# Sums of the norms by ones times the split total, and means by a masked sum on DVE

## The chip, the cores and the metric

One core of a Trainium2 chip runs the whole program. The metric is the device time of one execution in microseconds, as the median of several runs. The engines are named as in the profile: PE (TensorE, matrix products; PEld is its weight load), DVE (VectorE), ACT (ScalarE), POOL (GpSimd) and SP (SyncE, which issues the DMAs).

## What is computed

Two layers over 256 tokens of 1024 channels. Each layer has four residual steps, and each step starts with an RMS norm of x; a fifth norm stands behind the last layer:

```python
def rmsnorm(x, g):
    y = x * lax.rsqrt(jnp.mean(x * x, axis=-1, keepdims=True) + EPS)
    return y * g

for i in range(DEPTH):                                     # DEPTH = 2
    x = x + 0.5 * swiglu(rmsnorm(x, norm_ff1[i]), ...)     # norm 0, D_FF = 2816
    x = x + token_mixer(rmsnorm(x, norm_mix[i]), ...)      # norm 1: sparse attention and gated linear attention
    x = x + 0.5 * swiglu(rmsnorm(x, norm_ff2[i]), ...)     # norm 2
    g = sigmoid(rmsnorm(x, norm_ple[i]) @ ple_w_gate[i])   # norm 3
    x = x + g * (p[i] @ ple_w_proj[i])
return rmsnorm(x, norm_final)
```

All is float32, and 216 MB of weights are read once.

## The kernel before

x lies transposed in SBUF: channels on the 128 partitions, eight tiles of 128 x 256 tokens. The weights come in chunks of 128x2048 (1 MB) through three slots. For each chunk SP loads `raw`, ACT rounds it into `w_hi` (float32r, `split` at line 856), DVE puts the remainder into `w_lo` (`split` at line 1222), and PE makes three products of each pair of tiles, hi with hi, lo with hi, hi with lo (lines 385 to 387). x times the gain is split in the same way (lines 876 and 1248). A chunk's slot is used again for the chunk three further on, so the instruction `split(L, n + 3)` appears beside the work on chunk n. Each engine runs its own list of instructions in the order written; semaphores connect the lists.

The factor 1/rms of a token is not needed before the products: they run on x times gain, and their results are multiplied by `rb`, a 128x256 tile that holds each token's factor on all partitions. A norm k of layer L makes `rb` so:

1. ACT squares the tiles of x in pairs (line 866), POOL adds the eight squared tiles into `total` (128x256, lines 1149 and 1150) and counts `sq_added`.
2. PE, in `token_sums`, waits for `sq_added` and sums `total` over the partitions: two float32 products with `total` as the stationary operand and one column of ones, so that a token's sum stands on a partition, in 128x2 of PSUM (line 424).
3. DVE, in `mean_square`, makes `mean` of it (line 1261), POOL raises it to the power -1/2 (`rstd`, line 1152), and DVE puts the two halves of `rstd` on diagonals, split as `diag_hi` and `diag_lo` (lines 1267 and 1270).
4. PE, in `spread`, multiplies `ones_r` (128x128 ones) with both diagonals, 256 columns each (lines 434 and 435); ACT copies the result into `rb` (line 892).

Where the steps stand on PE: in norm 0 of layer 0 (`first`) the sums come in the third chunk, after its first column tile; in norms 0 and 2 otherwise within the second chunk; in norm 1 between the two chunks of `av`; in norm 3 behind the chunk of `PROJ`. Where they stand on DVE: in norms 0 and 2, `mean_square` comes between `split(L, n + 3)` and `split(L, n + 4)` of the first pair of chunks; in norms 1 and 3 it comes at the end of the feed-forward stage before, at its last chunk (c = 10), after the last `rest_pair` and ahead of that chunk's `split(L, n + 3)`.

Of the kernel before, what the change touches and what calls it, by code (L numbers as in the profile page):

```python
# [7 lines left out]
F32 = mybir.dt.float32  # L8
F32R = mybir.dt.float32r
ACT = mybir.ActivationFunctionType  # L10
ALU = mybir.AluOpType
AX_X = mybir.AxisListType.X

P = 128
EPS = 1e-6
# [17 lines left out]
T = 256  # L33
D = 1024
# [53 lines left out]
def hybrid_trunk(nc, a, out):  # L88
    L_N = a["gla_gate_w2"].shape[0]
    with ExitStack() as ctx:  # L90
        def sb(name, shape, dt=F32):

            line = 16
            held = ctx.enter_context(nc.sbuf_tensor(name, [*shape[:-1], -(-shape[-1] // line) * line], dt))
            return held[(slice(None),) * (len(shape) - 1) + (slice(0, shape[-1]),)]

        def sem(name):
            return ctx.enter_context(nc.semaphore(name))

        psum = ctx.enter_context(nc.psum_tensor("psum", [P, 8, 512], F32))  # L100
        bank = [psum[:, b, :] for b in range(8)]
# [19 lines left out]
        total = sb("total", [P, T])  # L121
        diag_hi = sb("diag_hi", [P, 2, P], F32R)
        diag_lo = sb("diag_lo", [P, 2, P], F32R)
        diag = total.rearrange("p (a t) -> p a t", a=2)
        ones_r = sb("ones_r", [P, P], F32R)
        ones = ones_r.bitcast(F32)
        w2 = sb("w2", [P, 256])
# [16 lines left out]
        mean = sb("mean", [P, 2])  # L144
# [50 lines left out]
        ident = consts[:, 0:P]  # L195
# [3 lines left out]
        def both(t):  # L199

            return t.unsqueeze(1).to_broadcast([P, 2, t.shape[-1]])
# [25 lines left out]
        sq_done = sem("sq_done")  # L227
        sq_added = sem("sq_added")
        sums_done = sem("sums_done")
        mean_done = sem("mean_done")  # L230
        rstd_done = sem("rstd_done")
        diag_rounded = sem("diag_rounded")
# [53 lines left out]
        START = 1  # L286
# [9 lines left out]
        def turn(L, n, g=0):  # L296

            return n % SLOTS, L * TURNS + n // SLOTS + g + 1
# [14 lines left out]
        def of_norm(L, k, pair):  # L313

            return (L * 4 + k) * 4 + pair
# [60 lines left out]
        def _(pe):  # L376
# [42 lines left out]

            def token_sums(L, k, b):  # L420

                pe.wait_ge(sq_added, of_norm(L, k, 4) + START)
                for t in range(2):
                    mm = pe.matmul(bank[b][:, T + t:T + t + 1], total[:, t * P:(t + 1) * P], ones[:, 0:1], start=True, stop=True)  # L424
                mm.then_inc(sums_done, 1)

            def spread(L, k, b):

# [9 lines left out]
            def ffn(L, off, f, h):  # L438
# [14 lines left out]
                for m in range(4):  # L453
                    if m == 3 and not first:
                        token_sums(L, k, 4)
                    if f == 0:
                        if m < 3:
                            pe.wait_ge(next_lo, L * 3 + m + 1)
                        else:
                            operands(L, off + 1)  # L460
                    for c in range(2):
                        mm = pairs(s, 2, h, c, (2 * m, 2 * m + 1))
# [367 lines left out]
            for c in range(3):  # L830
                if c:
                    pe.wait_ge(last_squares, c)
                for t in range(2):
                    half = slice(t * P, (t + 1) * P)
                    mm = pe.matmul(bank[4][:, T + t:T + t + 1], last_squared[:, c - 1, half] if c else total[:, half], ones[:, 0:1],
                                   start=c == 0 and t == 0, stop=c == 2, skip_group_check=True)
# [372 lines left out]
        def _(dve):  # L1209
# [8 lines left out]
            def split(L, n, g=0):  # L1218

                s, t = turn(L, n, g)  # L1220
                dve.wait_ge(hi_ready[s], t)
                dve.tensor_tensor(w_lo[:, s, :], raw[:, s, :], w_hi[:, s, :].bitcast(F32), ALU.subtract).then_inc(lo_ready[s], 1)  # L1222

            def chunk_products(L, n, g=0):
                s, t = turn(L, n, g)
                dve.wait_ge(chunk_done[s], t + START)
# [17 lines left out]
            def rest_pair(L, k, m, h):  # L1244

                dve.wait_ge(h_hi_ready, of_norm(L, k, m + 1))
                for c in (2 * m, 2 * m + 1):
                    ins = dve.scalar_tensor_tensor(out=h[1][:, c, :], in0=x[:, c, :], scalar=gains[:, k, c:c + 1],
                                                   in1=h[0][:, c, :].bitcast(F32), op0=ALU.mult, op1=ALU.subtract)
                ins.then_inc(h_ready, 1)  # L1250

            def add_half(L, m, first):

                xs = x[:, 2 * m:2 * m + 2, :]
                dve.scalar_tensor_tensor(out=xs, in0=high(first), scalar=0.5, in1=xs, op0=ALU.mult, op1=ALU.add
                                         ).then_inc(x_done, 1)

            def mean_square(L, k, b):

                dve.wait_ge(sums_done, L * 4 + k + 1)  # L1260
                dve.tensor_scalar(mean[:, :], bank[b][:, T:T + 2], 1.0 / D, EPS, ALU.mult, ALU.add).then_inc(mean_done, 1)
                dve.wait_ge(rstd_done, L * 4 + k + 1)
                roots = rstd[:, :].unsqueeze(2).to_broadcast([P, 2, P])
                if L * 4 + k == L_N * 4:
                    dve.tensor_tensor(diag[:, :, :], both(ident), roots, ALU.mult).then_inc(diag_done, 1)
                    return
                dve.tensor_tensor(diag_hi[:, :, :], both(ident), roots, ALU.mult).then_inc(diag_rounded, 1)
                dve.wait_ge(diag_rounded, L * 4 + k + 1)
                for t in range(2):
                    ins = dve.scalar_tensor_tensor(out=diag_lo[:, t, :], in0=ident, scalar=rstd[:, t:t + 1],  # L1270
                                                   in1=diag_hi[:, t, :].bitcast(F32), op0=ALU.mult, op1=ALU.subtract)
                ins.then_inc(diag_done, 1)

            def products(q):
                return high(2 * q) if q < 2 else tiles(UP_BANKS[(q - 2) % 6])

            def ffn(L, off, f, k, h):
                F = L * 22 + f * 11
                for g in range(N_FF):
                    n = off + 2 * g  # L1280
                    if g == 0:
                        split(L, n + 3)
                        if L == 0 and f == 0:
                            dve.wait_ge(const_landed, 16)
                        mean_square(L, 2 * f, 4)
                        split(L, n + 4)
                        dve.wait_ge(rb_ready, L * 4 + 2 * f + 1)
                    chunk_products(L, n)
                    dve.tensor_tensor(gate_sum, products(2 * g), both(rb), ALU.mult).then_inc(gate_scaled, 1)
                    if g:  # L1290
                        split(L, n + 3)
                    chunk_products(L, n + 1)
                    dve.tensor_tensor(up_sum, products(2 * g + 1), both(rb), ALU.mult).then_inc(up_scaled, 1)  # L1293
                    dve.wait_ge(up_scaled, F + g + 1)
                    dve.wait_ge(silu_done, F + g + 1)
                    dve.tensor_tensor(gated_up, up_sum, gate_act, ALU.mult).then_inc(hidden_done, 1)
                    if g:
                        split(L, n + 4)
                    dve.wait_ge(hidden_hi, F + g + 1)
                    dve.tensor_tensor(hid[1][:, 2 * g:2 * g + 2, :], gated_up, hid[0][:, 2 * g:2 * g + 2, :].bitcast(F32),  # L1300
                                      ALU.subtract).then_inc(hidden_lo, 1)
                for c in range(N_FF):
                    n = off + DOWN + c
                    if c in (2, 5, 8, 10):
                        m = (2, 5, 8, 10).index(c)
                        if m < 3:
                            dve.wait_ge(acc_ready, L * 6 + 3 * f + m + 1)
                        else:
                            chunk_products(L, n)
                        add_half(L, m, DOWN_BANKS[m])  # L1310
                        rest_pair(L, k, m, h)
                        if m == 3:
                            mean_square(L, k, 6 if f == 0 else 7)
                    split(L, n + 3)
                    if f == 1 and c == 0:
                        dve.wait_ge(p_hi, L + 1)
                        dve.tensor_tensor(small_lo[:, 2, :], p_in, small_hi[:, 2, :].bitcast(F32), ALU.subtract).then_inc(p_lo, 1)
# [323 lines left out]
            for i in range(2):  # L1641
                dve.wait_ge(x_landed[i], 16)
                for m in (2 * i, 2 * i + 1):
                    dve.wait_ge(h_hi_ready, of_norm(0, 0, m + 1))
                    for c in (2 * m, 2 * m + 1):
                        ins = dve.scalar_tensor_tensor(out=hB[1][:, c, :], in0=x[:, c, :], scalar=first_gains[:, c:c + 1],
                                                       in1=hB[0][:, c, :].bitcast(F32), op0=ALU.mult, op1=ALU.subtract)
# [106 lines left out]
```

## Time and profile before

| | us |
|---|---|
| median of three runs | 1180.99 (1180.85 to 1181.42) |
| span of the profiled execution | 1179.5 |
| PE busy | 1168.9 (99%) |
| DVE busy | 814.0 (69%) |
| ACT busy | 593.7 (50%) |
| POOL busy | 122.8 (10%) |
| DMA | 218.87 MB, 186 GB/s on average |

The span runs from the first to the last instruction of the profiled execution; the medians come from runs without the profiler's page. Products on PE are pipelined: each lasts 0.28 us in the records, while the next starts 0.11 us after it, so the starts tell what a product costs. In a timeline, several instructions of one form that follow each other are merged into one row with their count, and a bracket gives the idle time of the engine ahead of them and what ended it.

### The profile page before, as it was taken

Reading aid. Unit: us, or ns where it says so; the run is one execution under the profiler, and the core shown is the slowest. Engines: PE = TensorE matmul, PEld = TensorE weight load, DVE = VectorE, ACT = ScalarE, POOL = GpSimd, SP = SyncE. Lnnn points to the kernel's source line nnn. Section 1 sums busy time; section 2 is a strip of 40 time slices with the busy share of each in tenths; the row PEclk is TensorE's granted clock in tenths of the full one; section 3 lists DMA queues with packets and bytes.
Section 4 is the critical chain, followed back from the end, with each engine's and each line's share of the span. In section 5 each row is a group of like instructions: output and inputs, shape, how many; then the busy total and the mean of one; then the engine's idle time right before and its main releaser. Section 6 shows DMA issues by size and latency. Waiting matters only on the chain.

```text
span 1179.5 us, 24037 instructions
## 1 busy us (share of the span) xinstructions
PE 1168.9 (99%) x10534; PEld 1144.7 (97%) x10534; DVE 814.0 (69%) x939; ACT 593.7 (50%) x669; POOL 122.8 (10%) x136
## 2 busy tenths in 40 slices
PE   9999999999999999999999999999999999999997
PEld 9999999999999999999999999999899999999996
DVE  5866555688978766655786665558798777666455
ACT  5544445555745544444554444447367455444443
POOL 2000001011512000001210000100133020000011
PEclk9999999999999999999999999999999999999998
DMA  7655555545445555555555555554635365555541
GB/s 288 235 203 188 193 201 177 184 156 202 145 149 207 190 188 206 183 204 187 179 202 194 194 199 184 197 203 139 214 140 169 118 235 203 184 204 186 186 172 36
DMA packets 33384, 218.87 MB, mean 186 GB/s; under 512 B 5184, under 2 KB 6016, under 8 KB 7296
## 3 DMA queue, kind: packets, MB, share of 16 engines
q1 hardware_dynamic: 33280, 217.34, 53.2%
q8 instruction: 83, 1.36, 0.5%
q14 instruction: 21, 0.17, 0.0%
HBM read 216.15 MB, written 1.05 MB: 184 GB/s over the span
## 4 chain that ended last, share of the span: by engine, by line
PE 98%; DVE 1%; DMA 1%; ACT 0%; issue 0%; POOL 0%; SPq 0%; POOLq 0%; DVEq 0%
PE psum L385 31%; PE psum L387 31%; PE psum L386 31%; PE psum L665 1%; PE psum L644 1%; DMA x_all<-in_x 1%; PE psum L517 0%; PE psum L578 0%; PE psum L628 0%; PE psum L699 0%; PE psum L424 0%; PE psum L710 0%; PE psum L613 0%; DVE gates L1671 0%; PE psum L733 0%
## 5 line engine op out<-in xcount | busy, mean ns | idle before, releaser
L1222 DVE TENSOR_TENSOR w_lo<-raw,w_hi 128x2048 fp32r<-128x2048 f32 x200 | 457.9, 2293 | 213.5 <-ACT w_hi L856 213.4
L856 ACT ACTIVATE w_hi<-raw 128x2048 fp32r<-128x2048 f32 x201 | 385.2, 1917 | 366.6 <-PE psum L387 360.8
L385 PE MATMUL psum<-hA_hi,w_hi 128*128 128x256 f32 x1360 | 377.9, 278 | 0.0
L386 PE MATMUL psum<-hA_hi,w_lo 128*128 128x256 f32 x1360 | 375.7, 276 | 0.0
L387 PE MATMUL psum<-hA_lo,w_hi 128*128 128x256 f32 x1360 | 375.7, 276 | 0.0
L385 PEld LDWEIGHTS psum<-hA_hi,w_hi 128*128 128x128 f32 x1360 | 255.4, 188 | 2.7 <-issue 2.7
L386 PEld LDWEIGHTS psum<-hA_hi,w_lo 128*128 128x128 f32 x1360 | 255.4, 188 | 0.0
L387 PEld LDWEIGHTS psum<-hA_lo,w_hi 128*128 128x128 f32 x1360 | 255.3, 188 | 0.0
L385 PE MATMUL psum<-hB_hi,w_hi 128*128 128x256 f32 x832 | 230.3, 277 | 1.1 <-DVE w_lo L1654 1.1
L386 PE MATMUL psum<-hB_hi,w_lo 128*128 128x256 f32 x832 | 229.7, 276 | 0.0
L387 PE MATMUL psum<-hB_lo,w_hi 128*128 128x256 f32 x832 | 229.7, 276 | 0.0
L387 PE MATMUL psum<-hid_lo,w_hi 128*128 128x256 f32 x704 | 194.3, 276 | 0.0
L385 PE MATMUL psum<-hid_hi,w_hi 128*128 128x256 f32 x704 | 194.3, 276 | 0.0
L386 PE MATMUL psum<-hid_hi,w_lo 128*128 128x256 f32 x704 | 194.3, 276 | 0.0
L385 PEld LDWEIGHTS psum<-hB_hi,w_hi 128*128 128x128 f32 x832 | 156.2, 188 | 1.6 <-DVE w_lo L1654 1.5
L386 PEld LDWEIGHTS psum<-hB_hi,w_lo 128*128 128x128 f32 x832 | 156.2, 188 | 0.0
L387 PEld LDWEIGHTS psum<-hB_lo,w_hi 128*128 128x128 f32 x832 | 156.2, 188 | 0.0
L386 PEld LDWEIGHTS psum<-hid_hi,w_lo 128*128 128x128 f32 x704 | 132.2, 188 | 0.0
L387 PEld LDWEIGHTS psum<-hid_lo,w_hi 128*128 128x128 f32 x704 | 132.2, 188 | 0.0
L385 PEld LDWEIGHTS psum<-hid_hi,w_hi 128*128 128x128 f32 x704 | 132.2, 188 | 0.0
L1146 POOL TENSOR_TENSOR total<-silu 128x256 f32<-128x256 f32 x9 | 10.3, 1145 | 588.6 <-ACT silu L866 588.6
L1293 DVE TENSOR_TENSOR gates<-psum,rb 128x512 f32<-128x512 f32 x44 | 30.4, 690 | 39.7 <-PE psum L387 39.7
(182 smaller groups left out, 1226.0 us busy)
## 6 DMA issues: line engine op xcount, KB each, us to landing
raw<-in_weights SPq DMA_DIRECT2D x203, 1024.0 KB, 4.9
raw<-in_weights SPq DMA_DIRECT2D x2, 512.0 KB, 6.2
out<-gates SPq DMA_DIRECT2D x3, 256.0 KB, 2.2
x_all<-in_x SPq DMA_DIRECT2D x1, 520.0 KB, 3.9
x_all<-in_x SPq DMA_DIRECT2D x1, 512.0 KB, 6.2
relu<-in_p SPq DMA_DIRECT2D x2, 256.0 KB, 5.0
consts<-in_consts SPq DMA_DIRECT2D x1, 384.0 KB, 5.7
out<-gates SPq DMA_DIRECT2D x2, 128.0 KB, 2.3
```

Source lines behind the costliest of these rows:

```text
L385: pe.matmul(o, lh, rh, start=start, stop=False)
L386: pe.matmul(o, ll, rh, start=False, stop=False)
L387: return pe.matmul(o, lh, rl, start=False, stop=stop)
L644: mm = pe.matmul(bank[BANK_OF[f"oa{n}"]][64 * r:64 * r + 64, i * P:(i + 1) * P], v[:, kt, h * 64:(h + 1) * 64], probT[r][:, q * P:(q + 1) ...
L665: mm = pe.matmul(bank[BANK_OF[f"lv{p}{hh}"]][64 * c:64 * c + 64, first + q * cols:first + (q + 1) * cols], kk[rows, q * P + 64 * c:q * P + ...
L856: act.activation(w_hi[:, s, :], raw[:, s, :], ACT.Copy).then_inc(hi_ready[s], 1)
L1146: pool.tensor_tensor(total[:, :], squared[:, 0, :], squared[:, 1, :], ALU.add).then_inc(sq_added, 1)
L1222: dve.tensor_tensor(w_lo[:, s, :], raw[:, s, :], w_hi[:, s, :].bitcast(F32), ALU.subtract).then_inc(lo_ready[s], 1)
L1293: dve.tensor_tensor(up_sum, products(2 * g + 1), both(rb), ALU.mult).then_inc(up_scaled, 1)
```

## The change

For the eight norms within the layers, the sums are made with the operands exchanged: `ones_r` is stationary and `total` is moving, so that every partition gets the sums of all 256 tokens. To run as float32r, `total` is split by DVE into `total_hi` and `total_lo` (which use the memory of the diagonals), and eps goes into `total_lo`. `token_sums` on PE waits for the new semaphore `total_split` in place of `sq_added`. `mean_square` then takes each token's mean out of the 128x256 result by two scalar_tensor_tensor instructions, which multiply 128x128 with the identity and sum along the row. The final norm keeps its form. On DVE the order changes: in norms 0 and 2 `split_total` comes ahead of `split(L, n + 3)`, in norm 0 of layer 0 behind it; in norms 1 and 3 `split(L, n + 3)` comes first, then `split_total` and `mean_square`.

```diff
+        total_hi, total_lo = (t.rearrange("p a t -> p (a t)") for t in (diag_hi, diag_lo))
...
             def token_sums(L, k, b):
-                pe.wait_ge(sq_added, of_norm(L, k, 4) + START)
-                for t in range(2):
-                    mm = pe.matmul(bank[b][:, T + t:T + t + 1], total[:, t * P:(t + 1) * P], ones[:, 0:1], start=True, stop=True)
-                mm.then_inc(sums_done, 1)
+                pe.wait_ge(total_split, L * 4 + k + 1)
+                pe.matmul(bank[b][:, T:2 * T], ones_r[:, :], total_hi[:, :], start=True, stop=False)
+                pe.matmul(bank[b][:, T:2 * T], ones_r[:, :], total_lo[:, :], start=False, stop=True).then_inc(sums_done, 1)
...
+            def split_total(L, k):
+                dve.wait_ge(sq_added, of_norm(L, k, 4) + START)
+                dve.tensor_copy(total_hi[:, :], total[:, :]).then_inc(total_rounded, 1)
+                dve.wait_ge(total_rounded, L * 4 + k + 1)
+                dve.scalar_tensor_tensor(out=total_lo[:, :], in0=total[:, :], scalar=D * EPS / P, in1=total_hi[:, :].bitcast(F32),
+                                         op0=ALU.add, op1=ALU.subtract).then_inc(total_split, 1)
+
             def mean_square(L, k, b):
                 dve.wait_ge(sums_done, L * 4 + k + 1)
-                dve.tensor_scalar(mean[:, :], bank[b][:, T:T + 2], 1.0 / D, EPS, ALU.mult, ALU.add).then_inc(mean_done, 1)
+                if L * 4 + k == L_N * 4:
+                    dve.tensor_scalar(mean[:, :], bank[b][:, T:T + 2], 1.0 / D, EPS, ALU.mult, ALU.add).then_inc(mean_done, 1)
+                else:
+                    for t in range(2):
+                        half = slice(t * P, (t + 1) * P)
+                        ins = dve.scalar_tensor_tensor(out=total[:, half], in0=bank[b][:, T + t * P:T + (t + 1) * P], scalar=1.0 / D,
+                                                       in1=ident, op0=ALU.mult, op1=ALU.mult, accum_out=mean[:, t:t + 1])
+                    ins.then_inc(mean_done, 1)
...
                     if g == 0:
+                        if L or f:
+                            split_total(L, 2 * f)
                         split(L, n + 3)
                         if L == 0 and f == 0:
+                            split_total(L, 2 * f)
                             dve.wait_ge(const_landed, 16)
                         mean_square(L, 2 * f, 4)
...
                         rest_pair(L, k, m, h)
-                        if m == 3:
-                            mean_square(L, k, 6 if f == 0 else 7)
                     split(L, n + 3)
+                    if c == 10:
+                        split_total(L, k)
+                        mean_square(L, k, 6 if f == 0 else 7)
```

## Rows read from the trace of the kernel before

**Rows 1.** The page: chain that ended last, by engine.
```profile
PE 98%; DVE 1%; DMA 1%; ACT 0%; issue 0%; POOL 0%; SPq 0%; POOLq 0%; DVEq 0%
```

**Rows 2.** Waits of PE: who waited for whom, us in total, times, longest.
```profile
PE psum L431 <- DVE total L1265: 1.5, 1, 1.5
...
PE psum L835 <- ACT relu L1083: 0.3, 1, 0.3
```

**Rows 3.** Timeline of PE (start us, us, engine line), sums of norm 2.
```profile
389.83 0.50 PE L424 MATMUL psum<-ones_r,total 128*128 128x1 f32 x4
...
390.40 0.28 PE L386 MATMUL psum<-hA_hi,w_lo 128*128 128x256 f32 x1
```

**Rows 4.** Timeline of all engines, sums of the first norm.
```profile
22.24 0.60 PE L424 MATMUL psum<-ones_r,total 128*128 128x1 f32 x4
22.37 2.29 DVE L1222 TENSOR_TENSOR w_lo<-raw,w_hi 128x2048 fp32r<-128x2048 f32 x1 [3.92 <-ACT w_hi L856]
```

**Rows 5.** Timeline of PE, the spread of norm 1.
```profile
200.68 0.28 PE L434 MATMUL psum<-diag_hi,ones_r 128*128 128x256 f32 x1
...
200.91 0.28 PE L385 MATMUL psum<-hA_hi,w_hi 128*128 128x256 f32 x1
```

**Rows 6.** DVE by line and by shape (min/median/max ns, or busy us and mean ns).
```profile
L1620 DVE SCALAR_TENSOR_TENSOR x_all<-gates,x_all x4: 425/426/646, 588.9 to 1169.8; 128x256 f32<-128x256 f32 x4
...
L1344 DVE TENSOR_SCALAR selbias<-score 128x256 f32<-128x256 f32 x2 | 0.6, 296 | 0.1
...
L1465 DVE COPY state<-psum 128x256 f32<-128x256 f32 x2 | 0.8, 416 | 0.0
...
L1526 DVE SCALAR_TENSOR_TENSOR iqT<-psum,grstd,gsilu x16: 341/343/352, 337.9 to 919.7; 128x128 f32<-128x128 f32 x16
```

**Rows 7.** Timelines of DVE, POOL and PE, norm 0 of layer 1.
```profile
595.94 4.48 DVE L1222 TENSOR_TENSOR w_lo<-raw,w_hi 128x2048 fp32r<-128x2048 f32 x2
...
598.22 0.50 PE L424 MATMUL psum<-ones_r,total 128*128 128x1 f32 x4
...
600.57 0.71 POOL L1152 TENSOR_TENSOR rstd<-mean,half_neg 128x2 f32<-128x2 f32 x1 [5.71 <-DVE mean L1261]
...
601.31 0.43 DVE L1267 TENSOR_TENSOR diag_hi<-consts,rstd 128x256 fp32r<-128x256 f32 x1 [0.82 <-POOL rstd L1152]
601.77 0.61 DVE L1270 SCALAR_TENSOR_TENSOR diag_lo<-consts,rstd,diag_hi 128x128 fp32r<-128x128 f32 x2
...
602.77 0.28 PE L434 MATMUL psum<-diag_hi,ones_r 128*128 128x256 f32 x1
```

**Rows 8.** Timeline of all engines, norm 1 of layer 0.
```profile
191.43 1.90 ACT L856 ACTIVATE w_hi<-raw 128x2048 fp32r<-128x2048 f32 x1
...
192.60 0.74 POOL L1150 TENSOR_TENSOR total<-total,silu 128x256 f32<-128x256 f32 x1
...
194.70 0.50 PE L424 MATMUL psum<-ones_r,total 128*128 128x1 f32 x4
...
197.21 4.49 DVE L1222 TENSOR_TENSOR w_lo<-raw,w_hi 128x2048 fp32r<-128x2048 f32 x2
```

**Rows 9.** Timeline of PE, the first product behind a wait.
```profile
8.01 0.38 PE L385 MATMUL psum<-hB_hi,w_hi 128*128 128x256 f32 x1 [0.90 <-DVE w_lo L1654]
```

**Rows 10.** Timelines of ACT and PE, norm 3 of layer 0.
```profile
562.81 1.91 ACT L856 ACTIVATE w_hi<-raw 128x2048 fp32r<-128x2048 f32 x1
...
565.99 0.50 PE L424 MATMUL psum<-ones_r,total 128*128 128x1 f32 x4
```

**Rows 11.** Timeline of DVE, norm 2 of layer 0.
```profile
385.04 2.29 DVE L1222 TENSOR_TENSOR w_lo<-raw,w_hi 128x2048 fp32r<-128x2048 f32 x1 [1.45 <-ACT w_hi L856]
```

**Rows 12.** Stretches: length, busy us of each engine (instructions), granted clock, DMA share, GB/s.
```profile
2.00:3.00 1.00, 1.00 (x6) 1.00 (x6) 0.00 (x0) 0.78 (x2) 0.00 (x0) 1.00 0.63 191
...
5.00:6.00 1.00, 1.00 (x11) 1.00 (x11) 0.36 (x1) 1.00 (x4) 0.00 (x0) 1.00 0.72 225
...
1172.00:1172.50 0.50, 0.00 (x0) 0.00 (x0) 0.19 (x1) 0.00 (x0) 0.28 (x1) 0.52 0.00 0
```

More of the change, by code:

```diff
@@ L229, in hybrid_trunk @@
         sums_done = sem("sums_done")
+        total_rounded = sem("total_rounded")
+        total_split = sem("total_split")
         mean_done = sem("mean_done")
```

## The prediction, made before the change had run

> **What bounds the kernel now.** I read the chain of waits first: it runs through PE for 98% of the span [rows 1]. A busy PE alone says little, so next I read what PE waited for. Five rows answer that, 5.1 us in all: the warm-up, the first weights and three in the final norm; the first and the last row stand in [rows 2]. Between the first weights and the final norm PE waits for nothing. So every microsecond that the change takes from PE's own stream comes off the end, and every wait that it puts on PE is paid in full, since no later wait absorbs it. DVE, ACT and POOL are free as long as they stay ahead of PE. The question is: what do the sums cost on PE, and is DVE's new work done when PE arrives?
>
> **What comes off PE.** The old sums of a norm are two f32 products of one column, which the trace shows as four instructions. From their start to the second product behind them is 389.83 to 390.40, 0.57 us, where one product's spacing of 0.11 would be due: 0.46 us of PE [rows 3]. In the first norm the four last 0.60 instead of 0.50, so 0.56 there [rows 4]. The new sums are two f32r products of `ones_r` with 256 columns, the form that `spread` has already. Its pair holds PE from 200.68 to 200.91, 0.23 us [rows 5]. If nobody waits, each norm gives back 0.23 us and the first 0.33: 1.9 us over the eight.
>
> **What goes onto DVE ahead of PE.** PE used to wait for `sq_added` from POOL; now it waits for `total_split`, which DVE gives after a copy and a subtraction of 128x256. The subtraction is a scalar_tensor_tensor with a constant: 0.43 us, and once in four 0.65 [rows 6]. No row shows a copy of that size within SBUF. The nearest are a one-source tensor_scalar within SBUF, 0.30 us, and a copy out of PSUM, 0.42 [rows 6]. I take 0.30, because both its operands lie in SBUF as here; the bounds are 0.15 (half of it, an estimate) and 0.42. The Trainium skill (VectorE: DVE Perf Modes, section "Mode 2×_2P — use both read ports for one tensor") says that one-source f32 operations within SBUF run at two elements a cycle, and that PSUM has one read port only; by it the tensor_scalar is the right neighbour, and by the PSUM row each wait below would be 0.12 us longer. A hand-over from one engine or instruction to the next takes 0.03 to 0.04 us (600.57 + 0.71 to 601.31; 601.31 + 0.43 to 601.77 [rows 7]); I take 0.04. Without a wait DVE starts 0.09 us before the end of a 2.29 us split, as two of them take 4.48 [rows 7]. So from the end of a split that stands ahead, PE can start after -0.09 + 0.30 + 0.04 + 0.43 + 0.04 = 0.72 us.
>
> **What stands ahead on DVE, norm by norm.** Here the change loses.
>
> Norms 1 and 3, behind a feed-forward stage. The split of chunk n+3 used to follow `mean_square`; now it precedes `split_total`. DVE can begin it when ACT has rounded the chunk, 191.43 + 1.90 + 0.04 = 193.37, and ends it at 195.66. POOL's total is there at 192.60 + 0.74 = 193.34, but DVE is then in the split. PE could start the sums at 195.66 + 0.72 = 196.38 and arrives at 194.70 [rows 8]: it stands for 1.68 us. Its first product after standing lasts 0.38 instead of 0.28 [rows 9], 0.10 more. So norm 1 costs 1.68 + 0.10 + 0.23 - 0.46 = +1.55 us; layer 1 has the same pattern. In norm 3, 562.81 + 1.91 + 0.04 + 2.29 + 0.72 = 567.77 stands against an arrival at 565.99 [rows 10]: 1.78 us, hence +1.65. Two layers: 3.10 + 3.30 = 6.40 us.
>
> Norm 0 of layer 0. Here too the split comes first. It runs from 22.37 to 24.66, so the sums start at 25.38, and PE arrives at 22.24 [rows 4]: 3.14 us. 3.14 + 0.10 + 0.23 - 0.56 = +2.91 us.
>
> Norm 0 of layer 1. `split_total` comes between two splits. The second began at 595.94 + 4.48 - 2.29 = 598.13, so copy and subtraction end at 598.90, PE starts at 598.94 and arrives at 598.22 [rows 7]: 0.72 us, +0.59 in sum. A second wait follows. The other split now runs from 598.81 to 601.10, and only then come the means: two masked sums of 128x128 out of PSUM in place of one small instruction. A row of that shape without the sum takes 0.34 [rows 6], two overlapped 0.61 (at 601.77 [rows 7]). No row shows the sum along a row; I bound it by nothing and by 0.6 more for both, and take nothing, as nearest. The means end at 601.62, POOL's root (0.04 + 0.71) at 602.37, the diagonal (0.04 + 0.46 + 0.61) at 603.48, and PE may spread at 603.52. It comes there at 602.77 + 0.59 = 603.36 [rows 7], stands for 0.16 us and restarts, +0.26. Together +0.85.
>
> Norm 2. The split ahead ends at 385.04 + 2.29 = 387.33 [rows 11]; the split total is there at about 388.0, before PE's 389.83 [rows 3]. Nothing waits: -0.23 twice, -0.46.
>
> **What is hidden.** In norms 1 to 3 the longer means lie under products. In norm 1 the sums end at about 196.8, the means at 197.5, root and diagonal are there at 199.4; PE comes to the spread 6.0 us after the sums (194.70 to 200.68 [rows 5, 8]), at 202.2 with its wait. The cover is 2.8 us; if it were gone, PE would stand for what is missing. Of the two splits that stood behind the diagonal, 4.49 us from 197.21 [rows 8], one is left there and ends at 201.6 as before; uncovered, the chunk behind would be late by up to 2.29 us. SP may reload the other's raw buffer some 4 us sooner, which gives nothing, as PE waits for no load there. ACT's `rb` and all behind it move with PE. The final norm is unchanged and moves by the sum.
>
> **The sum.** 2.91 + 6.40 + 0.85 - 0.46 = +9.70 us. The profiled span is 1179.5 us; the median, 1180.99, lies 1.49 above it, which I leave as it is. 1180.99 + 9.70 gives **1190.7 us**. Bounds, on the six waits for the sums: copy 0.15 instead of 0.30, -0.90, or 0.42, +0.72; subtraction 0.65, +1.32; the seven restarts free, -0.70; the dear masked sum, +0.6. So 1189.1 to 1193.3 for this case.
>
> **The rivals.**
> - *No wait: the split total is ready when PE comes.* Only the 1.9 us come off, 1179.1 us, within what can be told. It decides at 194.70 in norm 1: DVE's subtraction would have to end before. For it speaks that POOL's total is there 1.36 us ahead of PE [rows 8], while copy and subtraction need 0.77. Against it: DVE works in the order written, and that has a 2.29 us split between. Chance 0.05.
> - *The clock falls in the long stand.* PE would stand for 3.14 us in the first norm. The granted clock is 0.52 on average from 1172.0 to 1172.5 [rows 12], after PE had waited again and again in the final norm [rows 2], so idle time takes it from 2.4 to 1.2 GHz here. The wait of 0.90 us before 8.01 [rows 9] did not slow the products behind it. Price: the warm-up issued 6 products a microsecond at first and 11 later (the column reads 1.00 for both) [rows 12]; 3 to 4 us at 6/11 of the rate lose 1.6 us, and twice that if it lasts twice as long. That gives 1192.3 to 1193.9. The Trainium skill (TensorE: Matmul & The Clock Gate, section "Why this matters for your kernels") warns of idle gaps between bursts of products, since a long one brings back the lower clock; by that warning the first stand is in danger and the shorter ones less. Chance 0.17.
> - *The waits are longer than read*, because copy or masked sum leave their bounds or a chunk behind comes late: 1193 to 1198. Chance 0.06.
> - *The forecast*: 0.72.
>
> **How the numbers follow.** The range takes in the forecast's bounds, a little below them (1188.5), and the clock's fall, to 1194.0. Left out are the case without waits and the longest waits, 0.11, and some of the fall, under 2 in 10. A measurement here can tell about 0.2%, 2.4 us. Slower by more: 0.72 + 0.17 + 0.06 = 0.95, of which I keep 0.02 back for waits that come only in part. Within: 0.05 with that. Faster would need more than the 1.9 us of the case without waits: 0.02.
>
> **What would show it.** Right: PE's waits list the new products, released by DVE's split of the total, near 3.1, 1.7, 1.8, 0.7, 1.7 and 1.8 us in order of time, and the spread of layer 1's norm 0 near 0.2; nothing in norm 2; a pair costs 0.23 us where nobody waits. Wrong: no such waits (then DVE's order is not what counts), a wait at a chunk of weights (a split came late), or a granted clock below 1.00 near 25 us. The most fragile term is the 3.14 us, which hangs on when ACT rounds that chunk behind POOL's slow additions.

## The result

| | kernel before | changed kernel |
|---|---|---|
| median, us | 1181.01 (1180.85 to 1181.42, four runs) | 1192.41 (1190.94 to 1192.62, four runs) |
| ratio, 95% interval | | 1.0091 (1.0079 to 1.0103) |
| span of the profiled execution, us | 1179.5 | 1190.5 (its own time 1192.28) |
| mean granted clock | 0.997 | 0.995 |

The change makes the kernel slower by 11.4 us, inside the range, 1.7 us above the predicted time. Where the time went is read off PE's waits. Of the changed kernel (who waited for whom, us in total, times, longest):

```profile
PE psum L426 <- DVE diag_lo L1265: 9.8, 6, 3.0
PE psum L433 <- DVE total L1282: 1.5, 1, 1.5
PE psum L825 <- POOL ones_r L1157: 1.2, 1, 1.2
PE psum L388 <- DVE w_lo L1675: 1.1, 2, 0.9
PE psum L837 <- POOL total L1152: 1.0, 1, 1.0
PE psum L837 <- ACT relu L1085: 0.2, 1, 0.2
```

The five lower rows are the waits that were there before, under new line numbers (their first and last are [rows 2]). The first row is new, and it is the change: six of the eight sums (line 426) wait for DVE's split of the total (line 1265, the subtraction; it writes `diag_lo`, whose memory `total_lo` uses). Here is norm 1 of layer 0 in the changed kernel, from its timelines of DVE, POOL and PE:

```profile
197.69 2.29 DVE L1224 TENSOR_TENSOR w_lo<-raw,w_hi 128x2048 fp32r<-128x2048 f32 x1 [1.45 <-ACT w_hi L858]
199.90 0.29 DVE L1263 CAST diag_hi<-total 128x256 fp32r<-128x256 f32 x1
200.22 0.43 DVE L1265 SCALAR_TENSOR_TENSOR diag_lo<-total,diag_hi 128x256 fp32r<-128x256 f32 x1
...
196.93 0.74 POOL L1152 TENSOR_TENSOR total<-total,silu 128x256 f32<-128x256 f32 x1
...
198.80 0.40 PE L390 MATMUL psum<-w_lo,hA_hi 128*128 128x512 f32 x1
200.71 0.39 PE L426 MATMUL psum<-diag_hi,ones_r 128*128 128x256 f32 x1 [1.51 <-DVE diag_lo L1265]
```

POOL's total is there at 197.67, PE comes at 199.03 (0.23 us after 198.80), and DVE begins the copy only at 199.90, when the weight split ahead of it is over. PE starts at 200.71, 1.68 us late. In [rows 8] the sums came at 194.70 without a wait. The bracket says 1.51, since the engine counts as busy until the modelled end of the product before; the distance of the starts is what PE loses.

One thing in the profile goes beyond the six waits. The first norm, timeline of PE and stretches (length, busy us of PE, PEld, DVE, ACT, POOL, granted clock, DMA share, GB/s):

```profile
22.10 0.28 PE L390 MATMUL psum<-hB_lo,w_hi 128*128 128x256 f32 x1
25.34 0.58 PE L426 MATMUL psum<-diag_hi,ones_r 128*128 128x256 f32 x1 [2.96 <-DVE diag_lo L1265]
25.71 0.42 PE L427 MATMUL psum<-diag_lo,ones_r 128*128 128x256 f32 x1
25.93 0.41 PE L388 MATMUL psum<-hB_hi,w_hi 128*128 128x256 f32 x1
26.15 0.41 PE L389 MATMUL psum<-hB_hi,w_lo 128*128 128x256 f32 x1
...
28.49 0.30 PE L388 MATMUL psum<-hB_hi,w_hi 128*128 128x256 f32 x1
28.64 0.28 PE L389 MATMUL psum<-hB_hi,w_lo 128*128 128x256 f32 x1
```
```profile
22.00:24.00 2.00, 0.38 (x4) 0.18 (x2) 1.67 (x1) 2.00 (x2) 0.12 (x1) 1.00 0.33 139
25.00:26.00 1.00, 0.66 (x3) 0.66 (x4) 0.28 (x1) 0.00 (x0) 0.00 (x0) 0.56 0.66 123
26.00:27.00 1.00, 1.00 (x6) 1.00 (x6) 0.51 (x4) 0.00 (x0) 0.17 (x1) 0.50 0.43 164
29.00:30.00 1.00, 1.00 (x11) 1.00 (x10) 1.00 (x1) 0.00 (x0) 0.00 (x0) 1.00 0.00 0
```

PE stands from 22.21 to 25.34, and when it goes on the granted clock is 0.50, 1.2 GHz: products start 0.21 us apart instead of 0.115, until 28.49. The pair and twelve products behind it take 3.15 us; at the full clock they would take 0.11 + 0.23 + 12 x 0.115 = 1.72. The fall costs 1.43 us. The sum of the profiled execution then closes: 2.91 (first norm) + 1.43 (clock) + 2 x 1.56 (norm 1) + 2 x 1.65 (norm 3) + 0.81 (norm 0 of layer 1) - 2 x 0.23 (norm 2) = 11.1 us, against 11.0 between the spans.

The fall seems not to be in every run: the run at 1190.94 us has a mean clock of 0.997, the three near 1192.5 have 0.995 or 0.996. Only one of the four was traced, the one at 1192.28. The mean clock alone is a weak sign, since every trace, that of the kernel before too, has a fall in the final norm, sooner or later in it ([rows 12] for the kernel before), and the kernel before has mean clocks from 0.996 to 0.998; the time is the better sign.

### The profile page after: what moved, and what is told of

Its sections match the earlier page's. It is cut to its first block, busy times and chain, and to the rows that moved or that the text cites. A ratio compares the mean times of both kernels' runs of the same rounds, so it can differ in the third digit from the quotient of the medians.

```text
span 1190.5 us, 24045 instructions
## 1 busy us (share of the span) xinstructions
PE 1170.3 (98%) x10518; PEld 1144.6 (96%) x10518; DVE 822.1 (69%) x979; ACT 593.3 (50%) x669; POOL 122.8 (10%) x136
## 4 chain that ended last, share of the span: by engine, by line
PE 92%; DVE 4%; ACT 2%; DMA 1%; issue 1%; POOL 0%; SPq 0%; POOLq 0%; DVEq 0%; ACTq 0%
PE psum L388 29%; PE psum L389 29%; PE psum L390 29%; DVE w_lo L1224 1%; ACT w_hi L858 1%; DMA raw<-in_weights 1%; PE psum L667 1%; PE psum L646 1%; PE psum L519 0%; PE psum L580 0%; PE psum L630 0%; PE psum L701 0%; ACT silu L868 0%; DVE w_lo L1243 0%; POOL total L1151 0%
```

## Experiments

Each ran beside the kernel before, experiments 1, 2, 3 and 6 on one chip and 4, 5 and 7 on another; its median was 1181.3 us on both.

**1. The first norm keeps the old sums.** Is the loss of the first norm what its stand and the clock behind it cost?

```diff
 def token_sums(L, k, b):
+    if L == 0 and k == 0:
+        pe.wait_ge(sq_added, of_norm(L, k, 4) + START)
+        for t in range(2):
+            mm = pe.matmul(bank[b][:, T + t:T + t + 1], total[:, t * P:(t + 1) * P], ones[:, 0:1], start=True, stop=True)
+        mm.then_inc(sums_done, 1)
+        return
...
                 split(L, n + 3)
                 if L == 0 and f == 0:
-                    split_total(L, 2 * f)
                     dve.wait_ge(const_landed, 16)
```

> The changed kernel, but norm 0 of layer 0 keeps the old sums and the old mean, so that DVE has nothing to give ahead of PE there. Theory (each wait costs what PE stands for, and the 3.1 us stand also lowers the clock): the stand of 3.13 us and the clock of 0.50 behind it both go, 0.11 + 0.23 - 0.56 of the products too, so 2.9 us plus 1.4 us less than 1192.4, near 1188.1 in every round, granted clock 1.00 near 25 us. Rival (the fall of the clock has nothing to do with the stand, or comes from the new products): the clock falls near 25 us or behind a later stand as well, 1189.5. Rival (a loss only moves on to a later chunk): over 1190.

Measured: 1188.40 us (1187.51 to 1188.44), ratio 1.0060 (1.0046 to 1.0074). Against the kernel before this is 7.1 us, where the changed kernel had 11.4: 4.3 us less, the 2.91 + 1.43 that the trace gave. Where the sums used to stand, the clock stays up, and it does so behind the five stands of 1.8 us and less that are left:

```profile
22.00:24.00 2.00, 2.00 (x19) 1.96 (x18) 1.51 (x1) 2.00 (x2) 0.29 (x1) 1.00 0.43 180
24.00:26.00 2.00, 2.00 (x20) 2.00 (x19) 1.17 (x3) 0.26 (x1) 0.72 (x1) 1.00 0.30 37
```

**2. Products that nobody reads fill the stand.** Does the clock fall because PE stands? DVE's work, and so the time at which the sums may start, stays the same.

```diff
 def token_sums(L, k, b):
+    if L == 0 and k == 0:
+        for _ in range(24):
+            pe.matmul(bank[5][:, 0:T], ones_r[:, :], hB[0][:, 0, :], start=True, stop=True)
     pe.wait_ge(total_split, L * 4 + k + 1)
```

> The changed kernel, with 24 products of 256 columns that nobody reads ahead of the sums of the first norm, 2.8 us of work inside the stand of 3.1 us. DVE is no sooner. Theory (idleness lowers the clock): PE waits for about 0.4 us instead of 3, the granted clock stays 1.00, and the time is that of the changed kernel without the fall, 1190.9 in every round. Rival (the clock falls for the weights' traffic or for the form of the products): the fall stays, 1192.3 or more, since the products behind still run at half rate.

Measured: 1190.97 us (1190.93 to 1191.35), ratio 1.0084 (1.0069 to 1.0100). The products fill 3.04 us, the sums start at 25.56, and behind them products start 0.12 us apart. Timeline of PE and stretches:

```profile
22.42 3.04 PE L427 MATMUL psum<-hB_hi,ones_r 128*128 128x256 f32 x24
25.56 0.38 PE L429 MATMUL psum<-diag_hi,ones_r 128*128 128x256 f32 x1
25.79 0.28 PE L430 MATMUL psum<-diag_lo,ones_r 128*128 128x256 f32 x1
25.91 0.28 PE L388 MATMUL psum<-hB_hi,w_hi 128*128 128x256 f32 x1
```
```profile
25.00:26.00 1.00, 0.89 (x7) 0.69 (x7) 0.47 (x2) 0.00 (x0) 0.00 (x0) 1.00 0.48 57
26.00:27.00 1.00, 1.00 (x11) 1.00 (x10) 0.51 (x4) 0.00 (x0) 0.23 (x1) 1.00 0.46 115
```

The same traffic, the same form of products, the same late start, and no fall: it is the idleness. The trace is that of one run, but all four lie within 1190.93 to 1191.35 us, where only one of the changed kernel's four does. Without the fall the change costs 1190.97 - 1181.31 = 9.7 us, the sum that had been worked out.

**3. In norms 1 and 3 the total is split first.**

```diff
+                    if c == 10:
+                        split_total(L, k)
                     split(L, n + 3)
                     if c == 10:
-                        split_total(L, k)
                         mean_square(L, k, 6 if f == 0 else 7)
```

> The changed kernel, but in norms 1 and 3 DVE does the split of the total before the split of chunk n+3. Theory (the split that stands ahead makes the wait): POOL's total is there about 1.3 us ahead of PE and DVE needs 0.75, so the four stands of 1.7 and 1.8 us vanish with their restarts: 2 x 1.79 + 2 x 1.88 = 7.3 us less, 1185.1 with the fall of the clock in the first norm, 1183.6 without. Rival (the hand-over through DVE itself is what costs): stands of some 0.7 us remain, 1187.5 or more. Rival (the split of the chunk now comes late): PE waits for weights at the next chunk, 2 us each, over 1190.

Measured: 1185.02 us (1183.49 to 1186.07), ratio 1.0031 (1.0019 to 1.0043). The four stands are gone: PE's wait for line 1265 is down from 9.8 us in six to 3.5 us in two, those of the norms 0.

```profile
PE psum L426 <- DVE diag_lo L1265: 3.5, 2, 3.0
```

In norm 1 (timelines of DVE and PE), DVE now waits for POOL and is done at 199.83, PE comes at 200.40 and goes straight on:

```profile
199.07 0.29 DVE L1263 CAST diag_hi<-total 128x256 fp32r<-128x256 f32 x1 [1.45 <-POOL total L1152]
199.40 0.43 DVE L1265 SCALAR_TENSOR_TENSOR diag_lo<-total,diag_hi 128x256 fp32r<-128x256 f32 x1
...
200.17 0.39 PE L390 MATMUL psum<-w_lo,hA_hi 128*128 128x512 f32 x1
200.40 0.28 PE L426 MATMUL psum<-diag_hi,ones_r 128*128 128x256 f32 x1
```

Neither rival holds: no stand of 0.7 us is left there, and no new wait for weights appears. Between runs without the fall, 1183.5 us stands against 1190.94 of the changed kernel: 7.4 us less, where 7.3 had been expected. The spread of the runs has two places, 1183.5 (mean clock 0.997, two runs) and 1185.0 to 1186.1 (0.995, three runs). The profiled one is of the second kind; its clock is low for longer than in the changed kernel:

```profile
24.00:25.00 1.00, 0.00 (x0) 0.00 (x0) 0.96 (x3) 0.14 (x1) 0.00 (x0) 0.77 0.00 0
25.00:26.00 1.00, 0.61 (x3) 0.61 (x4) 0.33 (x1) 0.00 (x0) 0.00 (x0) 0.50 0.60 82
30.00:31.00 1.00, 1.00 (x7) 1.00 (x6) 0.91 (x1) 0.00 (x0) 0.00 (x0) 0.50 0.00 0
32.00:33.00 1.00, 1.00 (x11) 1.00 (x10) 0.00 (x0) 0.00 (x0) 0.00 (x0) 1.00 0.81 147
```

**4. The order alone.** The kernel before with DVE's split of chunk n+3 ahead of the means in norms 1 and 3, and nothing else of the change.

```diff
                         rest_pair(L, k, m, h)
-                        if m == 3:
-                            mean_square(L, k, 6 if f == 0 else 7)
                     split(L, n + 3)
+                    if c == 10:
+                        mean_square(L, k, 6 if f == 0 else 7)
```

> The kernel before with one part of the change alone: at the end of both feed-forward stages DVE splits chunk n+3 ahead of the means; sums, operands and PE's wait are the old ones. Theory (the order costs only since PE now waits for what stands behind it): the means move by some 0.4 us, to about 195.7 instead of 195.2 in norm 1, the diagonal is still there before the spread, PE waits nowhere new: 1181.3 as the kernel before. Rival (the order in itself delays the chain to the spread or the next chunk): 1183 or more.

Measured: 1181.05 us (1180.70 to 1181.61), ratio 0.9998 (0.9989 to 1.0007). The order costs nothing while PE's sums wait for POOL; it costs 7.3 us, the four stands with their restarts, once they wait for an instruction that stands behind that split. With experiment 3 this closes the case for the four stands: neither the order nor the work of DVE costs alone, only both together.

**5. The old sums made three times.** What do they hold PE for?

```diff
-                for t in range(2):
+                for t in (0, 1, 0, 1, 0, 1):
                     mm = pe.matmul(bank[b][:, T + t:T + t + 1], total[:, t * P:(t + 1) * P], ones[:, 0:1], start=True, stop=True)
```

> The kernel before with each norm's old sums made three times over, 4 further products of one column, 8 instructions, in each of eight norms; the results are the same. Theory (four of these instructions hold PE for 0.36 us and 0.10 more is paid once behind them): 8 x 2 x 0.36 = 5.8 us more, 1187.1. Rival (the records overlap, and such instructions cost little beyond the change of form): under 1184. Rival (each costs the 0.25 us that it lasts): 8 x 8 x 0.25 = 16 us, 1197.

Measured: 1188.61 us (1188.37 to 1188.76), ratio 1.0062 (1.0049 to 1.0076). Sixteen further sets cost 7.3 us, 0.46 us each. The first expectation missed: the 0.10 us behind the sums are no single price for the change of form, they come with every set. In norm 2, twelve instructions and what is behind them hold PE from 391.64 to 393.10 less one spacing, 1.35 us, three times 0.45:

```profile
391.64 1.39 PE L424 MATMUL psum<-ones_r,total 128*128 128x1 f32 x12
392.90 0.36 PE L385 MATMUL psum<-hA_hi,w_hi 128*128 128x256 f32 x1
393.10 0.28 PE L386 MATMUL psum<-hA_hi,w_lo 128*128 128x256 f32 x1
```

So each one-column instruction holds PE as long as a product of 256 columns, 0.11 us, and the 0.46 us that the prediction took off PE per norm are confirmed from the time alone. Each of them brings a weight load of 128x128 of its own (PEld has twelve from line 424 in the same stretch); whether the load or the product sets the 0.11 us, no run tells.

**6. All waits taken away.** The new sums stay in seven norms. The first norm is as in experiment 1, norms 1 and 3 as in experiment 3, and in norm 0 of layer 1 the total is split ahead of both chunk splits and the means come between them.

```diff
                     for i in range(4):
                         next_piece(i)
+                    split_total(L + 1, 0)
                     split(L, PGATE + 6)
...
                     if g == 0:
-                        if L or f:
+                        if f:
                             split_total(L, 2 * f)
-                        split(L, n + 3)
+                        if L == 0 or f:
+                            split(L, n + 3)
...
                         mean_square(L, 2 * f, 4)
+                        if L and f == 0:
+                            split(L, n + 3)
                         split(L, n + 4)
```

> All three repairs: the first norm keeps the old sums, in norms 1 and 3 the split of the total comes ahead, and in norm 0 of layer 1 it comes ahead of both splits, with the means between them. Theory (without waits the new products give back 0.23 us a norm): PE waits nowhere between the first weights and the final norm, 7 x 0.23 = 1.6 us under the kernel before, 1179.4. Rival (the old sums cost nothing that comes back): 1181.0. Rival (a chunk's split is now late somewhere): a wait of PE for weights, 1181 to 1184.

Measured: 1179.51 us (1179.05 to 1179.95, eleven runs), ratio 0.9985 (0.9977 to 0.9994). This beats both kernels, if by little: 1.8 us (0.15%) under the kernel before, where 7 x 0.23 = 1.6 had been expected; its slowest run is faster than the fastest of the kernel before, 1180.72. PE waits nowhere between the first weights and the final norm:

```profile
PE psum L439 <- DVE total L1288: 1.5, 1, 1.5
PE psum L831 <- POOL ones_r L1163: 1.2, 1, 1.2
PE psum L843 <- POOL total L1158: 1.0, 1, 1.0
PE psum L388 <- DVE w_lo L1685: 0.5, 2, 0.3
PE psum L843 <- ACT relu L1091: 0.3, 1, 0.3
```

**7. The same, with the new sums in the first norm too,** the total split ahead of the chunk's split there.

> All repairs, and the first norm too has the new sums, with the split of the total ahead of the chunk's split. POOL's total is there just before PE comes, so PE stands for what DVE's two instructions and the hand-overs take, 0.74 us. Theory: 0.74 + 0.11 + 0.23 - 0.56 = +0.52 us against the version with the old sums there, 1180.0, granted clock 1.00 behind the stand in all rounds, since it is short. Rival (any stand can lower the clock): 1181 to 1182 in some rounds. Rival (the later split of the chunk makes a further wait): 1181 or more in all.

Measured: 1180.06 us (1179.61 to 1180.49, eleven runs), ratio 0.9990 (0.9982 to 0.9999), 0.55 us above experiment 6 (on the other chip) where 0.52 was expected. The stand is 0.70 us, and no run goes to the time of a fall. Timelines of PE and POOL:

```profile
22.17 0.28 PE L390 MATMUL psum<-hB_lo,w_hi 128*128 128x256 f32 x1
22.98 0.38 PE L426 MATMUL psum<-diag_hi,ones_r 128*128 128x256 f32 x1 [0.53 <-DVE diag_lo L1265]
...
21.39 0.74 POOL L1152 TENSOR_TENSOR total<-total,silu 128x256 f32<-128x256 f32 x1
```

In the first norm the old sums are the better ones: POOL's total comes just ahead of PE (22.13 against 22.28), and DVE's two instructions have nothing to hide behind.

## Why the prediction was right, step by step

- **PE has no slack.** Right. Every wait put on PE was paid in full at the end; the sum of the stands, restarts and products gives 11.1 us against 11.0 between the spans.
- **What comes off PE.** Right: 0.46 us a norm, by experiment 5 from the time alone. The new pair takes 0.23 where nobody waits, as in norm 2 of the changed kernel (timeline of PE, 395.71 to 395.94), and experiment 6 gives the difference back in seven norms (1.8 us, 1.6 expected).

```profile
395.71 0.28 PE L426 MATMUL psum<-diag_hi,ones_r 128*128 128x256 f32 x1
395.83 0.28 PE L427 MATMUL psum<-diag_lo,ones_r 128*128 128x256 f32 x1
395.94 0.28 PE L388 MATMUL psum<-hA_hi,w_hi 128*128 128x256 f32 x1
```

- **The price of DVE's two instructions.** Right. The copy takes 0.29 us (0.30 taken, from the SBUF row of [rows 6]), the subtraction 0.43 in all eight norms; the dear case of 0.65 never came. The neighbour that the Trainium skill (VectorE: DVE Perf Modes, section "Mode 2×_2P — use both read ports for one tensor") pointed to was the right one; the copy out of PSUM, 0.42, was not.
- **The stands.** Expected 3.14, 1.68, 1.78 and 0.72 us; measured 3.13, 1.68, 1.77 and 0.72. The waits for sums fell on the six norms named, and norm 2 has none. The reading that DVE works in the order written, and that the split ahead starts when ACT has rounded, carried all of it.
- **The second wait in norm 0 of layer 1.** There, and smaller than worked out: the spread starts 0.10 us late instead of 0.16. The two masked sums take 0.50 us (608.21 to 608.71) rather than 0.61; the sum along the row adds an instruction of 0.08 us to each, and the second sum starts beside the first of these. Timelines of DVE and PE of the changed kernel:

```profile
608.21 0.28 DVE L1276 SCALAR_TENSOR_TENSOR total<-psum,consts 128x128 f32<-128x128 f32 x1
608.41 0.08 DVE L1276 DVE_READ_ACCUMULATOR total<-psum,consts 128x1 f32 x1
608.41 0.28 DVE L1276 SCALAR_TENSOR_TENSOR total<-psum,consts 128x128 f32<-128x128 f32 x1
608.63 0.08 DVE L1276 DVE_READ_ACCUMULATOR total<-psum,consts 128x1 f32 x1
...
610.45 0.28 PE L390 MATMUL psum<-hB_lo,w_hi 128*128 128x256 f32 x1
610.66 0.39 PE L436 MATMUL psum<-diag_hi,ones_r 128*128 128x256 f32 x1
```

- **The clock.** Here the likeliest case was chosen wrongly. The prediction gave the fall 0.17; in the changed kernel it came, by the times, in three runs of four. Its mechanism was named (the first stand, not the shorter ones) and its price nearly right, 1.6 us against 1.43, though the 3 to 4 us for which it let the low clock last came from no row that it names: the profiled run has 3.2 us of slow products, that of experiment 3 has 6. The median, 1192.41, is that of this rival (1192.3 to 1193.9), not of the forecast. The run without it, 1190.94, and experiment 2, 1190.97 us, are the forecast's 1190.7. So it is in part luck that the time lies in the range: the forecast's own bounds (1189.1 to 1193.3) were for a dearer copy or subtraction, which did not come, and the case that did come was taken in as an unlikely one. The mistake was to weigh the fall by the 0.90 us wait of [rows 9], which was a third as long as the stand in question; the trace of before had no idle time of 3 us between products to weigh it by.

## What to carry to other kernels

Where one engine is busy from end to end, a saving on it counts only if what it waits for is ready when it arrives: read, for each new wait, what stands ahead of the releasing instruction on its own engine, and add it up to a tenth of a microsecond. Handing a sum through an additional engine is cheap (0.75 us here, hidden by 1.3 us of slack in norms 1 and 3) when its instruction is first in line, and dear (2.3 us more) behind a long one that nobody urgently needs. Before such a stand is left in a stream of products, ask whether it lasts long enough to bring down the clock.

## What the runs showed of the hardware

- A stand of PE of 3.1 us between full streams lowered the clock to 1.2 GHz in six of nine runs (three of four of the changed kernel, three of five in experiment 3); two of the six were traced, the others are told by the time and the mean clock. Single stands of 1.8 us and less in a full stream were never followed by a fall in a trace here. In the final norm, though, where PE stands again and again with few products between, the clock fell in every trace with no wait above 1.5 us ([rows 2] and [rows 12] for the kernel before): short stands close together did it too. How long it stays low differs: until 28.5 us in one profiled run, for 1.4 us of time, and until 31 in another, for 2.5 us against the runs without it. What decides whether it falls, and for how long, stays open.
- A one-column f32 instruction, with a 128x128 weight load of its own, holds PE for 0.11 us (experiment 5), as long as a 256-column f32r product; two f32 products of one column are dearer than two f32r products of 256.
- A copy of 128x256 from f32 to f32r within SBUF takes 0.29 us on DVE, where a two-source operation of that size takes 0.43.
